# Delta rule operands and the memory turned by VectorE blocks and DMA instead of TensorE transposes, and one convolution tap issued earlier

## The reference, cut to what matters

```python
def hybrid_mixer(xn, w_in, dn_conv_w, ...):
    proj = xn @ w_in
    qkv, z, b_raw, a_raw, glu = split(proj)
    qkv = silu(causal_depthwise_conv(qkv, dn_conv_w))       # 4 taps
    q, k, v = split(qkv)
    q, k = l2_normalize(q), l2_normalize(k)                 # 8 heads of 128
    beta = sigmoid(b_raw)
    g = -exp(dn_a_log) * softplus(a_raw + dn_dt_bias)
    o = chunk_gated_delta_rule(q, k, v, g, beta)
    ...
    c = causal_depthwise_conv(glu_a * sigmoid(glu_b), cf_dw_w) + cf_dw_b   # 31 taps

# inside the delta rule, chunks of 64 tokens, per head
g = cumsum(g)
decay = exp(where(causal, g[:, None] - g[None, :], -inf))
k_beta = k * beta
a    = (k_beta @ k.T) * decay
attn = (q @ k.T) * decay
u, w = triangular_solve(eye + strict(a), [v * beta, k_beta * exp(g)])

# cross-attention
k_mem, v_mem = rms_norm(mem) @ w_k, rms_norm(mem) @ w_v
```

## Time and profile before

| | |
|---|---|
| median of 3 runs | 2506.94 us (2506.9 to 2507.11) |
| the profiled execution: its own time | 2506.8 us |
| its span, first to last instruction | 2505.0 us |
| PE busy | 2490.8 us, 99% of the span |
| DVE, ACT, POOL busy | 1488.8, 1072.3, 104.7 us |
| transfers | 508.16 MB, 203 GB/s on average |
| granted PE clock | full (mean 0.999) |

### The profile page before, as it was taken

One profiled execution on the slowest core, in us unless ns is written; L12 is line 12 of the kernel. 1 busy time (PEld: TensorE's weight loads), 2 busy tenths in 40 slices (PEclk: granted clock), 3 DMA queues, 4 the chain that ended last, 5 costly groups with the idle time before them and its releaser, 6 DMA issues.

```text
span 2505.0 us, 28359 instructions
## 1 busy us (share of the span) xinstructions
PE 2490.8 (99%) x11953; PEld 2060.6 (82%) x11953; DVE 1488.8 (59%) x1275; ACT 1072.3 (43%) x883; POOL 104.7 (4%) x178
## 2 busy tenths in 40 slices
PE   9999999999999999999999999999999999999998
PEld 7888888888888888888888888877888888888887
DVE  5465655544456545678779996644655544456544
ACT  5444443333334334555454544533443433333333
POOL 0000000000000000122000002000000000000000
PEclk9999999999999999999999999999999999999999
DMA  8654666665566666787654457743766665566653
GB/s 301 208 187 137 210 227 211 210 210 193 196 215 221 226 195 208 216 288 204 204 167 146 162 189 237 227 144 128 219 217 218 219 198 189 198 203 233 222 198 134
DMA packets 160110, 508.16 MB, mean 203 GB/s; under 512 B 16128, under 2 KB 43920, under 8 KB 158704
## 3 DMA queue, kind: packets, MB, share of 16 engines
q1 hardware_dynamic: 153696, 485.35, 59.6%
q0 software_dynamic: 5872, 20.47, 2.6%
q10 hardware_dynamic: 416, 0.52, 0.1%
...
## 4 chain that ended last, share of the span: by engine, by line
PE 97%; DVE 1%; ACT 1%; DMA 0%; issue 0%; SPq 0%; POOLq 0%; POOL 0%; ACTq 0%
PE ps L840 31%; PE ps L841 30%; PE ps L844 30%; PE ps L1290 1%; PE ps L1306 1%; DVE weights_lo L1836 0%; PE ps L810 0%; DVE conv_out L2117 0%; PE ps L979 0%; DMA weights_raw<-in_w_in 0%; PE ps L1077 0%; PE ps L1050 0%; PE ps L1223 0%; PE ps L1211 0%; PE ps L873 0%; PE ps L862 0%
## 5 line engine op out<-in xcount | busy, mean ns | idle before, releaser
L1836 DVE TENSOR_TENSOR weights_lo<-weights_raw,weights_hi 128x2048 fp32r<-128x2048 f32 x431 | 986.3, 2289 | 883.0 <-ACT weights_hi L1370 883.0
L1370 ACT ACTIVATE weights_hi<-weights_raw 128x2048 fp32r<-128x2048 f32 x431 | 825.2, 1916 | 1172.7 <-PE ps L844 1121.9
L840 PE MATMUL ps<-weights_hi,stationary_hi 128*128 128x512 f32 x2408 | 944.6, 392 | 2.5 <-ACT stationary_hi L1387 1.2
L841 PE MATMUL ps<-weights_lo,stationary_hi 128*128 128x512 f32 x2408 | 937.3, 389 | 0.0
L844 PE MATMUL ps<-weights_hi,stationary_lo 128*128 128x512 f32 x2408 | 741.5, 389 | 0.0
L840 PEld LDWEIGHTS ps<-weights_hi,stationary_hi 128*128 128x128 f32 x2408 | 452.1, 188 | 98.6 <-issue 3.3
L844 PEld LDWEIGHTS ps<-weights_hi,stationary_lo 128*128 128x128 f32 x2408 | 452.0, 188 | 94.4
L841 PEld LDWEIGHTS ps<-weights_lo,stationary_hi 128*128 128x128 f32 x2408 | 452.2, 188 | 92.6 <-issue 0.5
L840 PE MATMUL ps<-weights_hi,hidden_hi 128*128 128x512 f32 x1008 | 392.1, 389 | 0.0
L841 PE MATMUL ps<-weights_lo,hidden_hi 128*128 128x512 f32 x1008 | 392.1, 389 | 0.0
L844 PE MATMUL ps<-weights_hi,hidden_lo 128*128 128x512 f32 x1008 | 310.2, 389 | 0.0
...
## 6 DMA issues: line engine op xcount, KB each, us to landing
weights_raw<-in_w SPq DMA_DIRECT2D x128, 1024.0 KB, 5.5
weights_raw<-in_w_in SPq DMA_DIRECT2D x79, 1024.0 KB, 5.6
weights_raw<-in_w_up SPq DMA_DIRECT2D x64, 1024.0 KB, 5.0
weights_raw<-in_w_down SPq DMA_DIRECT2D x64, 1024.0 KB, 5.6
weights_raw<-in_w_out SPq DMA_DIRECT2D x32, 1024.0 KB, 5.7
hidden<-turned_blocks SPq DMA_DIRECT2D x328, 64.0 KB, 2.8
weights_raw<-in_wk SPq DMA_DIRECT2D x16, 1024.0 KB, 5.6
weights_raw<-in_wv SPq DMA_DIRECT2D x16, 1024.0 KB, 5.5
```

The source lines that it names most:

```text
L840: pe.matmul(o, xh, WHI[:, slot, j, c * BANK:(c + 1) * BANK], start=first and j == 0, stop=False)
L841: pe.matmul(o, xh, WLO[:, low, j, c * BANK:(c + 1) * BANK], start=False, stop=False)
L1370: act.activation(WHI[:, s % NSPLIT], RAW[:, s % NRAW], ACT.Copy).then_inc(hi_ready, 1)
L1836: dve.tensor_tensor(WLO[:, s % NRAW], RAW[:, s % NRAW], WHI[:, s % NSPLIT].bitcast(F32), ALU.subtract).then_inc(lo_ready, 1)
```

## The change

The six turns by PE (convolved k; q, k and k·beta; the memory's two halves) go. In their place:

- "bk" (convolved k), "nk" and "nq" (normalised k and q), "mm0" and "mm1" (the memory's halves) are block rounds: two DVE instructions and 16 transfers each. ACT (and DVE for k) then reads the landed blocks from SBUF.
- k·beta is not turned. Beta is turned with the gate (one more small transpose), stored to HBM with it, and broadcast by two transfers straight into `KBT`; DVE multiplies the turned k into it. `DEC` now comes from rows of 256, so its broadcast is cut in pieces of 128 values too.
- the memory's tiles are split while pass gb runs and in wk0's first two steps, instead of in wk0 alone.
- PE no longer waits for k, q and k·beta at steps 2, 3 and 4 of ga; it waits for all of them before the grams.
- one tap of the 31 goes from wk1, step 3 to wk0, step 2.

```diff
+        RT_BK, RS_BK = back_blocks("turned_k", A0 + 56), back_blocks("hidden_k", A0 + 16)
+        RT_N, RS_N = at("turned_heads", [P, TT, COLS], A0 + 48), at("hidden_heads", [P, TT, P // SIDE, COLS // P, SIDE], A0 + 56)
...
-        GROWS = at("gate_rows", [P, P], slot(10) + 3)
-        scratch = nc.dram_tensor("gate_scratch", (U16, P), F32, kind="Internal").ap()
+        GROWS = at("gate_rows", [P, 2 * P], slot(10) + 3)
+        scratch = nc.dram_tensor("gate_scratch", (U16, 2 * P), F32, kind="Internal").ap()
...
-        MEM = at("memory", [P, TT, D], 0)
+        MEM = at("memory", [P, 2, TT, COLS], 0)
+        RT_M = at("turned_memory", [P, TT, COLS], slot(0))
+        RS_M = [MEM[:, n].rearrange("p t (i m r) -> p t i m r", i=P // SIDE, r=SIDE) for n in range(2)]
...
-        C31_TAPS = [0, 0, 0, 1, 1, 2, 2, 1] + [1] * PS + [1] * PS + [1, 1, 1, 1, 1, 1, 0, 1] + [1]
+        C31_TAPS = [0, 0, 1, 1, 1, 2, 2, 1] + [1] * PS + [1, 1, 1, 0, 1, 1, 1, 1] + [1, 1, 1, 1, 1, 1, 0, 1] + [1]
...
+        MEMORY_TILES = [range(0)] * 3 + [range(4), range(4, 6), range(6, 8), range(8, 10), range(10, 12), range(12, 14), range(14, 16)]
+
+        TURNED = {H_IN: 0, H_OUT: 8, H_OUT2: 16, H_XO: 20}
...
-            for n, name in enumerate(("cq", "ck", "cv", "bv"), 1):
-                load_pass(S_IN2 + n * PS, w_in2, IN2_COLS[n], 0, 5, lambda: move_by_sp(sp, name))
+            for n, names in enumerate((["cq"], ["ck"], ["cv", "bk"]), 1):
+                load_pass(S_IN2 + n * PS, w_in2, IN2_COLS[n], 0, 5, lambda: [move_by_sp(sp, name) for name in names])
+            for k in range(PS):
...
+                load_pass(S_IN2 + 4 * PS + k, w_in2, IN2_COLS[4], k, steps=1)
+                if k >= 5:
+                    move_by_sp(sp, ("nk", "bv", "nq")[k - 5])
...
-            load_pass(S_IN2 + 5 * PS, w_in2, IN2_COLS[5])
-            load_pass(S_KV, wk, 0, 0, 4, lambda: move_by_sp(sp, "gl"))
+            load_pass(S_IN2 + 5 * PS, w_in2, IN2_COLS[5], 0, 5, lambda: move_by_sp(sp, "mm0"))
+            for k in range(PS):
+                load(S_KV + k, blocks(wk)[k, :, :, 0:COLS])
+                if k in (0, 4):
+                    move_by_sp(sp, ("mm1", "gl")[k // 4])
...
+            move_by_pool(pool, "bk")
...
+            move_by_pool(pool, "nk")
             move_by_pool(pool, "bv")
 
-            pool.wait_ge(qk2_turned, 1)
             pool.wait_ge(gates_landed, 48)
-            pool.dma_start(DEC[:], scratch.partition_broadcast(P)).then_inc(gates_landed, 16)
+            for t in range(TT):
+                pool.dma_start(KBT[:, :, t * P:(t + 1) * P], scratch[t * HEADS:(t + 1) * HEADS, P:].partition_broadcast(P)).then_inc(gates_landed, 16)
+
+            pool.wait_ge(blocks_turned, turns("nq"))
+            pool.wait_ge(gates_landed, 80)
+            pool.dma_start(DEC[:], scratch[:, 0:P].partition_broadcast(P)).then_inc(gates_landed, 16)
+            move_by_pool(pool, "nq")
+            move_by_pool(pool, "mm0")
+            move_by_pool(pool, "mm1")
             move_by_pool(pool, "gl")
 
-            pool.wait_ge(turned, TURNED[H_MEM] + KT // 2)
+            pool.wait_ge(ht_hi, KT * (H_MEM + 1))
+            pool.wait_ge(ht_lo, KT * (H_MEM + 1))
...
-                    pe.transpose(ps[0:U16, 4, 0:P], gcs[:].rearrange("p t h -> p (t h)"), IDENT).then_inc(rows_ready, 1)
-
-            def during_z(k, j):
-                if (k, j) == (1, 0):
-                    left(P_IN2 + 2)
-                    pe.wait_ge(silu_ready, 2)
-                    turn_back(COUT, 0, conv_back)
...
-                if k == 2:
+                if k == 6:
+
                     left(P_IN2 + 3)
-                    pe.wait_ge(qn_ready, 1)
-                    turn_rows(lambda h, t: QTOK[:, t, h * HD:(h + 1) * HD], 1, qk2_turned)
-                elif k == 3:
-                    pe.wait_ge(qk2_ready, 1)
-                    pe.wait_ge(kn_ready, 1)
-                    turn_rows(lambda h, t: KTOK[:, t, h * HD:(h + 1) * HD], 1, qk2_turned)
-                elif k == 4:
                     pe.wait_ge(qk2_ready, 2)
                     pe.wait_ge(kb_ready, 1)
-                    turn_rows(lambda h, t: KB_[:, t, h, :], 1, qk2_turned)
-                elif k == 6:
-
-                    pe.wait_ge(qk2_ready, 3)
...
-            gemm_pass(S_IN2 + 3 * PS, P_IN2 + 3, during_z)
-            pe.wait_ge(sec0, 2)
-            pe.wait_ge(sec1, 2)
+            gemm_pass(S_IN2 + 3 * PS, P_IN2 + 3)
             gemm_pass(S_IN2 + 4 * PS, P_IN2 + 4, during_ga)
             gemm_pass(S_IN2 + 5 * PS, P_IN2 + 5, during_gb)
             pe.wait_ge(inv_a, 2)
             pe.wait_ge(inv_b, 2)
-            pe.wait_ge(mem_ready, 2)
-            first_pass(S_KV, P_KV, H_MEM, lambda k, t: MEM[:, t, k * P:(k + 1) * P], during_wk0)
+            gemm_pass(S_KV, P_KV, during_wk0, H_MEM)
...
-                if k in (2, 3, 4):
-                    act.wait_ge(qk2_turned, k - 1)
-                    dst = (QT2, KT2[:], KBT)[k - 2]
-                    act.activation(dst.rearrange("p h t -> p (h t)"), flat_high, ACT.Copy).then_inc(qk2_ready, 1)
+                if k in (2, 4):
+                    wait_landed(act, ("nk", "nq")[k // 4])
+                    act.activation((KT2[:], QT2)[k // 4].rearrange("p h (j r) -> p h j r", r=SIDE), RS_N[:].rearrange("p t i m r -> p m (t i) r"), ACT.Copy).then_inc(qk2_ready, 1)
...
+            def split_memory(n):
+                for k in MEMORY_TILES[n]:
+                    if k in (0, KT // 2):
+                        wait_landed(act, ("mm0", "mm1")[2 * k // KT])
+                    act.wait_ge(w_used, S_IN2 + 5 * PS + k // STEP + 1)
+                    act.activation(HHI[:, k, :].rearrange("p (j r) -> p j r", r=SIDE), RS_M[2 * k // KT][:, :, :, k % (KT // 2), :].rearrange("p t i r -> p (t i) r"),
+                                   ACT.Copy, scale=gain(G_MEM + k)).then_inc(ht_hi, 1)
...
-                    conv_store(KTOK, 0)
+                    dve.wait_ge(sq_done, TT * (N_MEM + 1))
+                    turn_conv("bk", 1)
                     sum_squares(0)
                 elif k == 2:
                     dve.wait_ge(rstd_ready, N_MEM + 1)
                     for t in range(TT):
-                        dve.tensor_scalar(MEM[:, t, :], MEM[:, t, :], rstd_of(N_MEM, t), None, ALU.mult).then_inc(mem_ready, 1)
+                        dve.tensor_scalar(MEM[:, :, t, :], MEM[:, :, t, :], rstd_of(N_MEM, t), None, ALU.mult).then_inc(mem_ready, 1)
                 elif 3 <= k < 3 + CONV:
+                    if k == 4:
+                        back_store(1, KTOK)
                     conv4_tap(2, k - 3)
+                    if k == 4:
+                        sum_squares(1)
                 elif k == 7:
-                    sum_squares(1)
+                    dve.wait_ge(l2_ready, 1)
+                    dve.tensor_tensor(heads(KTOK), heads(KTOK), l2_of(1), ALU.mult).then_inc(kn_ready, 1)
             for k in range(PS):
                 split_next(S_IN2 + 4 * PS + k)
                 if k == 0:
-                    turn_conv("bv", 2)
-                    dve.wait_ge(l2_ready, 1)
+                    dve.wait_ge(l2_sum, 2)
+                    dve.wait_ge(kn_ready, 1)
+                    turn("nk", KTOK, P_IN2 + 1)
                     dve.tensor_tensor(heads(QTOK), heads(QTOK), l2_of(0), ALU.mult).then_inc(qn_ready, 1)
                 elif k == 1:
-                    dve.tensor_tensor(heads(KTOK), heads(KTOK), l2_of(1), ALU.mult).then_inc(kn_ready, 1)
+                    turn_conv("bv", 2)
                 elif k == 2:
-                    dve.wait_ge(kn_ready, 1)
-                    dve.tensor_tensor(KB_[:], heads(KTOK), per_head(beta[:]), ALU.mult).then_inc(kb_ready, 1)
+                    dve.wait_ge(qn_ready, 1)
+                    turn("nq", QTOK, P_IN2)
                 elif k == 3:
+                    dve.wait_ge(gates_landed, 80)
+                    dve.wait_ge(qk2_ready, 1)
+                    dve.tensor_tensor(KBT, KBT, KT2[:], ALU.mult).then_inc(kb_ready, 1)
                     back_store(2, VTOK)
                 elif k == 4:
 
-                    dve.wait_ge(gates_landed, 64)
+                    dve.wait_ge(gates_landed, 96)
...
+            def turn_memory(half):
+                dve.wait_ge(mem_ready, 2)
+                dve.wait_ge(gram_ready, 2)
+                turn(("mm0", "mm1")[half], MEM[:, half], P_IN2 + 3)
+
+            def split_memory(n):
+                for k in MEMORY_TILES[n]:
+                    dve.wait_ge(ht_hi, KT * H_MEM + k // 2 * 2 + 2)
+                    dve.wait_ge(w_used, S_IN2 + 5 * PS + k // STEP + 1)
+                    dve.scalar_tensor_tensor(HLO[:, k, :].rearrange("p (j r) -> p j r", r=SIDE),
+                                             RS_M[2 * k // KT][:, :, :, k % (KT // 2), :].rearrange("p t i r -> p (t i) r"), gain(G_MEM + k),
+                                             HHI[:, k, :].bitcast(F32).rearrange("p (j r) -> p j r", r=SIDE), ALU.mult, ALU.subtract).then_inc(ht_lo, 1)
+
```

(33 more changed lines are left out.)

70 lines of the change are left out of this document (28 added, 42 removed).

## The result

The changed kernel takes 2516.75 us (median of 6 runs, 2512.78 to 2519.82) against 2506.92 (2506.13 to 2507.11): ratio 1.0038, interval 1.0028 to 1.0048, so slower by 9.8 us. The forecast was 2509.4, range 2501.5 to 2516.0. Both gaps have to be explained.

A forecast was written before the change was run, and what follows sets the result against it. PE was taken to bound the kernel (busy 99% of the span). Removed turns -11.3, late grams +10.7, grams to gb +3.1 gave +2.5 on the profiled 2506.8: 2509.3, or 2509.4 for the median; range 2501.5 to 2516.

The forecast's parts named there:

- What goes: PE's six turns removed, one small transpose added: net -11.3 us, 7.0 ahead of gb and 4.4 in the memory.
- The wait at step 5: In ga, PE waits about 8 us for a split queued behind beta's broadcast, taken to land at 1211.4.
- The grams: End of ga: grams start at 1223.9, after the decay's broadcast (1221.3), "nq" and q's copy; 10.7 us past due.
- From the grams to gb: DVE and ACT splits now stand behind q: 18.7 us instead of 15.6, so +3.1.
- Memory, gb, the tap: Rounds mm0 and mm1 come before they are read, loads no later, wk1's 1.1 us wait stays: cost 0.
- One number for the landings: Each broadcast of beta and decay in ga priced at 9.9 us, borrowed from a 1 MB table's load.
- The slow rival: Broadcasts of 13.0 us in ga, or a colder PE: grams at 1230.1, +8.7, 2515.7 us; chance 0.33.
- The clock: PE at half pace behind ga's waits: 4.8 us a step, mostly hidden after step 5's wait, not after the grams'.
- rules weighed: Skill's DMA rule: 512-byte pieces reach line rate, so broadcasts land in 8.5 us, total near 2506.6; clock rule: idle PE falls to 1.2 GHz.

The follow-up runs named there:

- e8: The kernel before with the memory part of the change alone, the tap left in wk1: 2502.84 us, ratio 0.9985.
- e1: The kernel before with the memory part and the moved tap; delta rule's operands still turned by PE: 2501.28 us, ratio 0.9979.
- e5: The changed kernel again, nothing altered, 10 runs and a second profile: 2514.11 us, ratio 1.0027.
- e2: The changed kernel with the memory turned by PE as before, its tiles split in wk0, the tap where it was: 2517.58 us, ratio 1.0041.
- e9: The changed kernel with the memory's second half turned in gb's step 2, not 3, and mm1 issued behind gb's last load: 2511.97 us, ratio 1.0024.
- e3: The changed kernel with beta's two broadcasts issued ahead of round nk, into v_tok's memory: 2509.57 us, ratio 1.0009.
- e14, e13: The changed kernel again, nothing altered, one more profiled execution: 2514.82 us.
- e6: The changed kernel with beta broadcast early, q turned by PE, v's store and ACT's copy of turned k a step later: 2499.23 us, ratio 0.9973.

## Why the prediction was wrong

By its own steps, against the first profile:

- **What goes.** -7.0 ahead of gb and -4.4 in the memory. Held in the main: without the tap the memory's part gained 3.8 (e8), with it 5.5 (e1). Behind gb's last matmuls the first profile is 4.45 shorter than before.
- **The wait at step 5.** 8 us forecast, 4.9 to 8.4 measured. KBT was there at 1208.7 instead of 1211.4: 7.5 us behind the first of its two issues, where the sum has about 10.6 (9.9 behind the second). The order of the queue and of DVE was read rightly.
- **The grams.** 1223.9 forecast, 1223.75 measured. That was luck, two errors that cancel: the decay landed 3.3 earlier (1218.0), and "nq" came 3.6 behind it (1221.6), not 0.7.
- **From the grams to gb.** 18.7 forecast, 18.6 measured. Up to here, +6.5 where +6.8 was counted.
- **"Memory, gb, the tap": cost 0.** This step failed. gb took 56.5 us instead of 52.5 (1298.87 - 1242.36 against 1288.42 - 1235.88). The stall is 2.5 of it, and about 1.5 come behind it, where `PEclk` reads 0.69 (1278 to 1283 us). I had looked at whether mm1 comes in time for its readers, not at what its transfers delay. For the profiled execution the forecast was 2509.3; with 4.0 more in gb, 0.3 less ahead of it and 0.1 less behind it that is 2512.9, against 2512.8. The 1.1 of the tap does not show in this total.
- **One number for the landings.** This failed too, and it carries the median out of the range. The sum goes by one broadcast time for all executions. They differ between executions: 8.7, 10.0, 10.7 and 12.6 us for the decay's. The slow rival's 13 us was nearly met in one profile of four, with grams at its 1230. Of the changed kernel's 18 executions three lie above the range's 2516.0, all among the first six; the ten of e5 have a median of 2514.1, inside it. That the landings are the rest, from the profiled 2512.8 to the first median of 2516.8, is inferred: none of the three was profiled. The two halves apart add up to 5.3 us more than before (10.8 less 5.5), about 2512.1. e2's profile has no stall, and e9's, which has none at that place either, comes to 2512.0; the changed kernel's two medians lie 2.0 and 4.7 above that sum. Why the landings differ was not tested by taking a neighbour away. SP's loads of 1 MB stand beside each broadcast. In the kernel before, e1 and e8, where POOL issues no round behind it, the decay's landed in 8.5, 8.6 and 8.0 us; in the changed kernel "nq" is issued right behind it. But so it is in e3, at 8.6.
- **The clock.** Behind step 5's wait half clock was to be "mostly hidden by the wait for q": held in the first profile. Behind the grams' wait it was not: the grams, 3.71 us there, took 5.38 in e5 and e14 and 6.60 in e13.

Of the rules weighed: the broadcasts in pieces of 512 bytes landed in 8.7 us at best in the changed kernel, and in 8.6 and 8.4 in e3 and e6, where 8 KB took 8.5. The Trainium skill ("DMA: Bandwidth & Descriptors", Specifications) is borne out as far as the piece goes. By it the total was 2506.6. It missed the same 4.0 us in gb as the forecast's own 9.9, so it would not have mended the result.
